# Opening loads of a fused decoder layer in order of use on one queue, first feed-forward units by arrival, and bulk transfers queued only behind few waiting bytes

## What is computed

```python
mod = (silu(c) @ w_ada + b_ada)            # 9 vectors of 1024: shift, scale, gate for 3 sub-layers
u = modulate(rmsnorm(h, ffn1_norm), sh1, sc1)
h = h + 0.5 * g1 * swiglu(u, ffn1_w_gate, ffn1_w_up, ffn1_w_down)     # 1024 -> 2816 -> 1024
u = modulate(rmsnorm(h, mix_norm), sh2, sc2)
h = h + g2 * hybrid_mixer(u, ...)          # 4 heads of differential + 4 of latent attention, causal
u = modulate(rmsnorm(h, ffn2_norm), sh3, sc3)
h = h + 0.5 * g3 * swiglu(u, ffn2_w_gate, ffn2_w_up, ffn2_w_down)
return rmsnorm(h, final_norm)
```

## Time and profile before

| | |
|---|---|
| median of 3 executions | 2810.1 us (2807.42 to 2811.35) |
| profiled execution | 2836.6 us, span of its slowest core (core 1) 2834.9 us |
| spans of the 8 cores in it | 2788.8 to 2834.9 us |
| TensorE (PE) busy, core 1 | 2716.7 us, 96% |
| VectorE, ScalarE, GpSimd busy | 54%, 42%, 20% |
| DMA | 523.63 MB, mean 185 GB/s |

### The profile page before, as it was taken

The page is one execution under the profiler, slowest core; times in us unless marked ns, Lnnn a source line. Parts: engine busy times, 40 slices in busy tenths (PEclk is TensorE's granted clock), DMA queues, the critical chain, the costliest instruction groups (busy, mean ns, idle before and its releaser), DMA issues.

```text
span 2834.9 us, 39739 instructions; the slowest of 8 cores (2788.8 to 2834.9 us)
## 1 busy us (share of the span) xinstructions
PE 2716.7 (96%) x15663; PEld 1354.1 (48%) x15663; DVE 1540.8 (54%) x3013; ACT 1180.2 (42%) x1962; POOL 572.2 (20%) x535
## 2 busy tenths in 40 slices
PE   3999999799999999999999999999999999999998
PEld 1444444344544555455554544454445545555443
DVE  3544267558557544673535775855755448343543
ACT  3311034333554455354653352345345633555411
POOL 1001111124024131402204206013131050040100
PEclk9999999888999999999999999999999999999999
DMA  9478869976996897786544664745555455435353
GB/s 207 106 144 154 191 150 250 248 210 173 235 260 215 186 271 189 225 236 185 178 161 151 231 190 151 238 140 179 194 169 199 143 178 182 132 127 187 121 186 117
DMA packets 150618, 523.63 MB, mean 185 GB/s; under 512 B 15520, under 2 KB 32288, under 8 KB 139168
## 3 DMA queue, kind: packets, MB, share of 16 engines
q1 hardware_dynamic: 133152, 459.94, 50.0%
q0 software_dynamic: 17280, 61.15, 14.5%
HBM read 479.10 MB, written 103.07 MB: 205 GB/s over the span
## 4 chain that ended last, share of the span: by engine, by line
PE 75%; DMA 12%; DVE 6%; POOL 4%; ACT 2%; issue 1%; SPq 0%; DVEq 0%; POOLq 0%; ACTq 0%
PE psall L368 75%; DVE mt L368 2%; POOL ac L368 2%; POOL sq L368 2%; DMA wm<-w_gu 1%; DMA mix<-w_ada 1%; DMA s_v<-mix 1%; DMA wf<-s_dn 1%; DMA s_gu<-wm 1%; DMA h<-xT 1%; DVE h L368 1%; DMA wf<-s_gu 1%; ACT pt L368 1%; DMA s_uq<-wm 1%; DMA wm<-s_in 1%
## 5 line engine op out<-in xcount | busy, mean ns | idle before, releaser
L368 PE MATMUL psall<-uF,wf 128*128 128x512 bf16 x5376 | 1438.8, 383 | 19.1 <-DMA wf<-s_gu 14.5
L368 PEld LDWEIGHTS psall<-uF,wf 128*128 128x128 bf16 x5376 | 514.1, 99 | 541.1 <-issue 47.5
L368 ACT ACTIVATE pt<-psall 128x512 bf16<-128x512 f32 (+3 forms) x896 | 484.9, 561 | 444.0 <-PE psall L368 440.4
L368 PE MATMUL psall<-actv,wf 128*128 128x512 bf16 x2464 | 626.0, 384 | 5.7 <-DMA wf<-s_dn 5.7
L368 DVE SCALAR_TENSOR_TENSOR ft<-ft,psall 128x512 f32<-128x512 f32 x352 | 240.5, 685 | 390.9 <-ACT ft L368 390.1
L368 ACT ACTIVATE ft<-psall 128x512 f32<-128x512 f32 x352 | 209.4, 596 | 483.0 <-PE psall L368 481.2
L368 PEld LDWEIGHTS psall<-actv,wf 128*128 128x128 bf16 x2464 | 236.9, 99 | 259.0 <-issue 27.2
L368 PE MATMUL psall<-mix,pt 128*128 128x129 bf16 x3264 | 334.9, 223 | 8.0 <-ACT pt L368 3.1
L368 PEld LDWEIGHTS psall<-mix,pt 128*128 128x128 bf16 x3264 | 251.1, 99 | 190.6 <-ACT pt L368 13.5
L368 DVE SCALAR_TENSOR_TENSOR h<-psall,SC,h 128x512 f32<-128x512 f32 x184 | 137.7, 749 | 320.2 <-PE psall L368 320.0
L368 DVE TENSOR_TENSOR actv<-ft,psall 128x512 bf16<-128x512 f32 x308 | 210.7, 684 | 167.6 <-PE psall L368 165.6
(11 more groups left out here) (131 smaller groups left out, 2102.1 us busy)
## 6 DMA issues: line engine op xcount, KB each, us to landing
wf<-s_gu SPq DMA_DIRECT2D x286, 512.0 KB, 4.9
wf<-s_dn SPq DMA_DIRECT2D x108, 512.0 KB, 4.2
wm<-s_in SPq DMA_DIRECT2D x63, 512.0 KB, 4.5
wf<-s_dn SPq DMA_DIRECT2D x54, 384.0 KB, 4.0
h<-s_h SPq DMA_DIRECT2D x16, 1024.0 KB, 7.9
outT<-h SPq DMA_DIRECT2D x16, 1024.0 KB, 4.9
h<-xT SPq DMA_DIRECT2D x14, 1024.0 KB, 14.3
s_h<-h SPq DMA_DIRECT2D x14, 1024.0 KB, 10.9
```

What stands on the lines that cost most here:

```text
L368: ins = getattr(eng, o.fn)(**o.kw)
```

## The change

1. The opening loads stand in one list, `OPENING`, all on GpSimd's queue: weights of fp 0, x of tile 1, weights of fp 1 and fp 2, x of tile 2; the two tiles of x in four parts of 512 KiB each.
2. The six write-backs of those weights, and the loads of lambda and positions, wait for the last transfer of that list.
3. The lead runs in the order of `UNITS`, and inside a unit `swiglu_pair` fills four banks with k as the outer loop.
4. Keys and values are stored in two halves of four heads, with a dependency each.
5. The planner's rates change, and it puts a transfer marked `bulk` on the SP queue only when at most 300,000 bytes are waiting in its model of that queue. Marked are spills, unspills, `store_u`, `store_o`, keys and values, and x of tiles 3 to 7.

```diff
-CAST_RATE = 262.0
+CAST_RATE = 275.0
 PLAIN_RATE = 400.0
-PLAIN_BESIDE_CAST = 215.0
+BACKLOG = 300000
...
         def speed(k):
-            return CAST_RATE if k else PLAIN_BESIDE_CAST if queues[True] else PLAIN_RATE
+            n = sum(1 for q in queues.values() if q)
+            return (CAST_RATE if k  else PLAIN_RATE) / max(n, 1)
...
+        def backlog():
+            return sum(b for _, b in queues[False]) + sum(o.nbytes * o.heavy for _, _, o in begin if o.eng != "pool")
...
+            elif e == "sp" and backlog() > BACKLOG:
+                ready = [x for x in avail[e] if not x[2].bulk]
+                if not ready:
+                    continue
+                pick = min(ready)
...
+OPENING = [('gu', 0), ('x', 1), ('gu', 1), ('gu', 2), ('x', 2)]
+UNITS = [(0, 0), (1, None), (0, 1), (1, 0), (1, 1), (2, None), (0, 2), (1, 2), (2, 0), (2, 1), (2, 2)]
...
+        def swiglu_pair(fp, wg, wgR, wu, wuR, u, uR, av, aR, bank):
+
+            banks = [(bank.next(), bank.next()) for c in range(2)]
+            for k in range(NK):
+                for c in range(2):
+                    for wt, wR, bk in ((wg, wgR, banks[c][0]), (wu, wuR, banks[c][1])):
+                        MM(bk, PS[bk], wv(wt)[:, k, c * 128:(c + 1) * 128], u[k], k == 0, k == NK - 1, [wR, uR[k]])
+            for c in range(2):
+                swiglu_act(2 * fp + c, *banks[c], av, aR)
...
-                G.dma("sp", "ks", 1048576, heavy=2.3, r=kstR, w=[s_kR[(sq, tt)]], out=s_k[sq][:, :, tt * 512:(tt + 1) * 512].rearrange("h p n -> p h n"), in_=kst)
+                for hs in (slice(0, 4), slice(4, 8)):
+                    G.dma("sp", f"ks{hs.start}", bulk=True, nbytes=524288, heavy=2.3, r=kstR[hs], w=[s_kR[(sq, tt, hs.start)]],
+                          out=s_k[sq][hs, :, tt * 512:(tt + 1) * 512].rearrange("h p n -> p h n"), in_=kst[:, hs, :])
...
+        held = []
+        wf.kept = []
+        with G.seg(-0.7, -0.6, "open", eng="pool"):
+            for what, i in OPENING:
+                if what == "gu":
+                    held.append(gu_load(0, i))
+                else:
+                    load_x(i, i - 1, 4, eng="pool")
+        begun = G.ops[-1]
+        with G.seg(-0.5, -0.4, "keep", eng="sp"):
+            for keep in wf.kept:
+                keep(after=begun)
+        wf.kept = None
```

More of the change, by code:

```diff
@@ L40 @@
     __slots__ = ("idx", "eng", "fn", "kw", "deps", "cost", "vt", "dma", "nbytes", "dsem", "grp", "dval", "nd", "succ",
-                 "ready", "start", "end", "pos", "inc", "tick", "table", "vc", "waits", "tag", "first", "port", "heavy")
+                 "ready", "start", "end", "pos", "inc", "tick", "table", "vc", "waits", "tag", "first", "port", "heavy", "bulk")
     def __init__(self, idx, eng, fn, kw, cost):
@@ L64, in __init__ @@
         self.heavy = 1.0
+        self.bulk = False
 class Graph:
@@ L116, in _link, with dma @@
             s.append(o)
-    def dma(self, eng, stream, nbytes, r=(), w=(), after=None, heavy=1.0, **kw):
+    def dma(self, eng, stream, nbytes, r=(), w=(), after=None, heavy=1.0, bulk=False, **kw):
         o = Op(len(self.ops), eng, "dma_start", kw, 530.0 if eng == "pool" else 450.0)
@@ L122, in dma @@
         o.heavy = heavy
+        o.bulk = bulk
         o.dsem = stream
@@ L226, in schedule @@
             for e in ENGS:
-                if avail[e]:
+                if e == "sp" and avail[e] and backlog() > BACKLOG and all(x[2].bulk for x in avail[e]):
+                    if not pend[e]:
+                        continue
+                    t = max(free[e], pend[e][0][0])
+                elif avail[e]:
                     t = free[e]
@@ L250, in schedule @@
             t, e = best
+            t = max(t, clock[0]) if e == "sp" else t
             while pend[e] and pend[e][0][0] <= t:
@@ L724, in table @@
             piR = posR
[L725 removed]
+            G.dma("sp", "pos", 128 * 2048, heavy=3.0, w=[piR], after=after, out=pi, in_=pos[b:b + 1, q * 512:(q + 1) * 512].broadcast_to([128, 512]))
             ang, angR = mtmp.next()
@@ L755, in cols, with load_x @@
             return slice(ks.start * 512, ks.stop * 512)
-        def load_x(t, s, n=2, after=None):
+        def load_x(t, s, n=2, after=None, eng="sp"):
             for st, ks, ap in parts(s, n):
-                G.dma("sp", f"x{s}{st}", 262144 * (ks.stop - ks.start), heavy=1.25, w=HR[s][ks], after=after, out=ap, in_=xT[t][:, cols(ks)])
+                G.dma(eng, f"x{eng[0]}{s}{st}", bulk=t > 2, nbytes=262144 * (ks.stop - ks.start), heavy=1.25, w=HR[s][ks], after=after, out=ap, in_=xT[t][:, cols(ks)])
         def squares(srcs, acs, sqs, ars):
@@ L833, in gate_up, with gate_up_first @@
                     swiglu_chunk(2 * fp + c, *w, c, uF, uFR, ACTV, actR, fb)
[L835 to L842, removed]
+        def gate_up_first(sets, first, hook):
+            for fp in range(first, 11):
                 w = gu_load(0, fp)
@@ L1170, in n1 @@
                 apply_norm(s, 0, t // 4, st, uF, uFR, ntmp)
-        with G.seg(0.0, 1.333, "F1.0-2g"):
-            gate_up_first(sets, 3, hook_j)
+        for n, (t, fp) in enumerate(UNITS):
+            if fp is None:
+                with G.seg(-0.2 + 0.05 * t, -0.15 + 0.05 * t, f"N1.{t}"):
+                    st = hstats(t - 1, jb.next())
+                    apply_norm(t - 1, 0, 0, st, *sets[t][0:2], ntmp)
+            else:
+                with G.seg(0.03 * n, 0.03 * n + 0.03, "F1.0-2g"):
+                    swiglu_pair(fp, *held[fp], *sets[t], jb)
+        with G.seg(0.33, 1.333, "F1.0-2g"):
+            gate_up_first(sets, len(held), hook_j)
         with G.seg(0.9, 0.95, "mixinit", eng="pool"):
@@ L1231, in build @@
         n1(3, A, 1.97)
-        ra(*mixers[0], work[0])
+        ra(*mixers[0], work.get(0, ()))
         n2(2, B, 2.0, True)
```

44 lines of the change are left out of this document (27 added, 17 removed).

## The result

The changed kernel took **2770.24 us** (median of four runs, the lowest three 2768.15 to 2772.12), the kernel before 2810.72 beside it (2807.42 to 2815.21). The ratio is **0.9852, 95% interval 0.9833 to 0.9872**: 41.6 us less of 2810.7. Forecast were 2788 and a range of 2774 to 2807. So the direction was right and the size was not: 22 us were forecast, and about 40 came.

A forecast was written before the change was run, and what follows sets the result against it. The prediction took matmuls on TensorE to bound the kernel, with only the opening and 400 to 575 us worth something. 17 + 5 = 22 us off the median 2810.1 gave 2788 us, range 2774 to 2807.

The forecast's parts named there:

- "5 us" for 400 to 575: 400 to 575 us: transfers put off past 575 us shorten TensorE's waits by 5 us, bounds 0 and 14.2.
- 14.2 us of waits: 400 to 575 us: TensorE's last three waits, on weight loads behind x, keys, `s_u` and values on SP; upper bound.
- the dip that the prediction set aside: 575 to 775 us, core 1: granted clock 0.86, costing 22 us, taken as untouched by the change.
- The later waits: After the middle stretch: waits for `s_dn`, 5.7 us in all, put at 0, between -3 and +3.
- "17 us" for the opening: Opening: fp 3 begins at 111.6 us in place of 129.0, a gain of 17.4, taken as 17.
- Ada's end: Opening: the last ada tile lands at 39.2 us, before at 41.41, as position and lambda loads leave the time ahead.
- the list's landing: Opening: tile 2 of x, last of the loads on GpSimd's queue, is in at 71.6 us.
- the costs that I set to nothing: Opening: eight extra issues on GpSimd's queue, six late write-backs (9.5 us of transfers) and four-bank evacuation, costed at nothing.
- "The bulk rule moves nothing": Middle stretch: another wait replaces each one removed, only the opening is gained, 2793 us; chance 0.20.
- "Uncast loads cost like casts": GpSimd's queue: x loads as slow as casts, opening gives 9.8 us, middle 1, 2799 us; chance 0.17.
- "Given back": Up to 1100 us: put-off transfers hold weight loads for about 12 us, opening gives 15, 2807 us; chance 0.11.
- "Slower": Six tiles: late keys and values hold ScalarE and VectorE, 5.3 us each, 32 in all, 2820 us; chance 0.10.

The follow-up runs named there:

- bulk_only: Kernel before with only the bulk rule, new planner rates and halved keys and values, opening as before: 2790.69 us, ratio 0.9902.
- old_rates: Changed kernel with the planner's rates of before, bulk rule and halves kept: 2798.09 and 2802.61 us, ratio 0.9941.
- no_split: Changed kernel with keys and values written whole, bulk rule and new rates kept: 2777.63 us, ratio 0.9862.
- late_wb: Changed kernel with the planner's rates of before, and what waits for a cast planned 8 us later: 2783.43 to 2788.5 us, ratio 0.9888.
- open_only: Kernel before with only the new opening list, late write-backs and four-bank units: 2800.0 and 2800.39 us.

## Why the prediction was wrong

**"5 us" for 400 to 575: the step that failed.** It measured about 25 us (27.6 for `bulk_only`, 25 between `old_rates` and the change), with what it brought up to 1100 us. Four things were wrong in it.
- *The limit taken was the wrong one.* I argued that "the engines are full for all 175 us", so that only what lands after 575 could help, and halved the 14.2 us of waits. The engines are full in the change too, at 1.01. What changed was which bytes come first, and how long SP's queue stands still for one transfer: PE's waits for transfers went from 17.6 to 2.6 us at the same share.
- *The planner's rates were left out.* The diff had them, three lines among many, and I gave them no term. `old_rates` shows them to decide: without them rule and halves are worth nothing in the middle.
- *The clock behind a wait was left out.* I had priced it in the opening, and not here. Core 7 before, TensorE:
```profile
513.60 2.74 PE L368 MATMUL psall<-uF,wf 128*128 128x512 bf16 x6 [6.17 <-DMA wf<-s_gu]
```
  The next row starts 2.54 us later, so the six matmuls take 0.42 us each and not 0.216, at the lower level, 1.2 GHz; granted clock was 0.86 from 500 to 525 us and 0.91 from 550 to 575 on this core, and 0.80 from 500 to 525 on cores 3 and 5. Cores 0 and 1 are left out here: they stay at 0.81 from 575 to 700 us with TensorE busy without a gap, which is the dip that the prediction set aside. On cores 2 to 7 the clock was 0.95 to 0.98 between 375 and 600 (mean 0.967), and 0.99 to 1.00 after the change. Over some 205 us busy that is, as an estimate, 7 us, more than half of what the idle time itself gave (20.7 to 7.8 us).
- *The later waits at 0, "between -3 and +3".* From 600 us on they gained 6 us up to 1100 and lost 3.5 behind it, the latter mostly on `uF<-s_o`. In the sum 2.5, within the bound, and by luck.

**"17 us" for the opening:** 14.2. Ada's end (38.1 for 39.2) and the list's landing (70.3 for 71.6) came a little before their forecasts. Left out were VectorE's 3.16 us ahead of unit (0, 1), part of the clock's cost behind it, and 2.9 us of tile 2's sums and `uF`, which had been in idle time. Of the costs that I set to nothing, the late write-backs and the issues on GpSimd's queue show none in the trace; the four banks bring nothing, and may cost 2 us.

**The rivals.** "The bulk rule moves nothing" (0.20): wrong for the kernel as changed (9 us by the ratios), and yet right with the old rates, so its argument was not foolish, only about another kernel. "Uncast loads cost like casts" (0.17): wrong, 6.3 us a tile. "Given back" (0.11): it exists, at 3.5 us and not 12, behind 1100 us. "Slower" by late keys and values (0.10): not seen, the change being faster; that the halves do no harm is all that `no_split` can say. No rival was on the side of a larger gain, though the idle time and the lower clock of that stretch, read together from the rows that I had, come to more than 20 us; the range ended at 2774 for that reason.

**What stays open:** how much of the 25 us the 18.75 us issue cost by itself (it goes with the rule or with the rates, but never alone), why it lasts so long, whether it is the write-backs by which the sharing helps, and the 10 us that `late_wb` leaves.

## What to carry to other kernels

Where a planner writes the order of an in-order queue, its rates are code as much as its rules are: with one too fast for two queues at once SP waited 97 us of 225 for casts here, with loads behind them, so a changed rate needs a term of its own in a forecast. Price an idle stretch of TensorE with the matmuls at the lower clock behind each wait, and bound its gain by all of that, not by the share of the DMA engines being full. And work that lay in idle time costs in full once the idle time is gone.

## What the runs showed of the hardware

- A DMA issue on SP, 0.32 to 0.38 us as a rule, can take 18.1 to 21.5 us (before, all eight cores), and 13.8 to 17.7 on a write-back in `open_only`, with no semaphore to wait for. Both stand behind x, `s_u`, keys and values with DMA share 1.0. That the queue was full is a guess; no run measured it by itself.
- Four parts of an uncast tile on GpSimd's queue ran at 333 GB/s, like SP's loads, and not at a cast's pace.
- A cast of 1 MiB, 3.3 us with the engines to itself, took 12 us from issue to landing beside SP's loads.
